# Forgetting attention: both heads of a pair through a query block together, scores as K=64 products in two row groups

## What is computed

```
logits = einsum('bhqd,bhkd->bhqk', qi, k) * scale + Fi[..., :, None] - F[..., None, :]
logits = where(kpos[None, :] <= qpos[:, None], logits, -inf)
p = softmax(logits, axis=-1)
out = einsum('bhqk,bhkd->bhqd', p, v)          # per head, swept over query blocks
y_f = out.reshape(B, S, F_W) * silu(f_z)
```

## Time and profile before

| | |
|---|---|
| median of 3 runs | 1825.53 us (1823.52 to 1827.44) |
| profiled execution | 1827.74 us, span 1826.1 us, mean granted clock 0.964 |
| TensorE busy | 1700.4 us (93%) |
| TensorE weight loads | 1301.9 us (71%) |
| VectorE busy | 826.4 us (45%) |
| ScalarE busy | 490.5 us (27%) |
| attention stage | first score at 1033.65 us, last output store issued at 1539.26 us |

### The profile page before, as it was taken

The page is one execution under the profiler, slowest core; times in us unless marked ns, Lnnn a source line. Parts: engine busy times, 40 slices in busy tenths (PEclk is TensorE's granted clock), DMA queues, the critical chain, the costliest instruction groups (busy, mean ns, idle before and its releaser), DMA issues. The chain is left out here.

```text
span 1826.1 us, 24542 instructions
## 1 busy us (share of the span) xinstructions
PE 1700.4 (93%) x8650; PEld 1301.9 (71%) x8650; DVE 826.4 (45%) x1819; ACT 490.5 (27%) x738; POOL 126.2 (7%) x122
## 2 busy tenths in 40 slices
PE   7689999999999999999998399999899996799998
PEld 6558888877777778888886266566565663688887
DVE  1942234221111134453111376566575664677774
ACT  1611011100010012221000255455454553322221
POOL 1610000000000000000000000000000000122221
PEclk9779999999999999999999699999999998799999
DMA  9520231321111111122111844506208101677762
GB/s 338 162 82 26 101 115 57 115 92 69 69 69 69 57 69 69 70 75 74 70 53 61 200 143 105 138 12 159 89 6 201 47 13 29 180 185 187 191 177 84
DMA packets 142094, 187.54 MB, mean 103 GB/s; under 512 B 9113, under 2 KB 116349, under 8 KB 135933
## 3 DMA queue, kind: packets, MB, share of 16 engines
q1 hardware_dynamic: 135252, 139.98, 27.8%
q0 software_dynamic: 6784, 46.89, 6.6%
HBM read 126.77 MB, written 60.06 MB: 102 GB/s over the span
## 5 line engine op out<-in xcount | busy, mean ns | idle before, releaser
L559 PE MATMUL a_ps_u<-a_h_hi,a_w_hi 128*128 128x512 f32 x1152 | 469.3, 407 | 0.0
L559 PE MATMUL a_ps_u<-a_h_lo,a_w_hi 128*128 128x512 f32 x1152 | 465.1, 404 | 0.0
L559 PE MATMUL a_ps_u<-a_h_hi,a_w_lo 128*128 128x512 f32 x1152 | 336.3, 406 | 0.0
L559 PEld LDWEIGHTS a_ps_u<-a_h_hi,a_w_hi 128*128 128x128 f32 x1152 | 216.6, 188 | 52.9 <-issue 1.9
L559 PEld LDWEIGHTS a_ps_u<-a_h_lo,a_w_hi 128*128 128x128 f32 x1152 | 216.7, 188 | 48.8
L559 PEld LDWEIGHTS a_ps_u<-a_h_hi,a_w_lo 128*128 128x128 f32 x1152 | 210.2, 188 | 51.2
L1213 DVE CUSTOM_DVE_ANT_0 f_probs<-f_ps_s,f_neg_f 128x512 f32<-128x512 f32 (+2 forms) x320 | 186.8, 608 | 130.3 <-PE f_ps_s L1101 80.4
L634 ACT ACTIVATE a_u_copy<-a_ps_u 128x2048 f32<-128x2048 f32 x28 | 52.8, 1886 | 462.9 <-PE a_ps_u L559 462.9
L1135 PE MATMUL f_ps_o<-f_probs_t,v_tok 128*64 128x512 f32 (+3 forms) x640 | 158.4, 559 | 13.4 <-ACT f_probs_t L1304 8.6
L1295 ACT ACTIVATE f_probs<-f_probs,f_neg_max 128x128 f32<-128x128 f32 (+15 forms) x128 | 153.5, 1199 | 54.5 <-DVE f_neg_max L1221 54.4
L1100 PE MATMUL f_ps_s<-k_hi,q_pack 128*128 128x512 f32 (+2 forms) x320 | 136.9, 428 | 19.3 <-DMA f_neg_f<-scratch_f_negF 13.4
(11 more groups left out here) (196 smaller groups left out, 1867.9 us busy)
## 6 DMA issues: line engine op xcount, KB each, us to landing
scratch_arrays<-a_stage POOLq DMA_DIRECT2D x27, 1024.0 KB, 4.2
a_w_land<-in_w_in SPq DMA_DIRECT2D x36, 512.0 KB, 3.8
scratch_qkT<-a_stage POOLq DMA_DIRECT2D x8, 2048.0 KB, 7.6
a_w_ring<-in_w_ada SPq DMA_DIRECT2D x12, 1024.0 KB, 9.0
a_x_ring<-in_x SPq DMA_DIRECT2D x16, 512.0 KB, 3.4
q_pack<-scratch_qkT SPq DMA_DIRECT2D x32, 256.0 KB, 7.5
k_hi<-scratch_qkT SPq DMA_DIRECT2D x32, 256.0 KB, 8.1
k_lo<-scratch_qkT SPq DMA_DIRECT2D x32, 256.0 KB, 8.6
```

The lines of the kernel that those rows point to most:

```text
L559: ins = pe.matmul(ps_u[:, par, b, :], w[:, k, :], h[:, k, cols], start=(k == 0 and i < 2 * len(blocks) and h is h_hi), stop=(k == KT - 1 a ...
```

## The change

Both heads of a pair now go through query group J together. Queries and keys lie as `q_hi`, `q_lo`, `k_hi`, `k_lo` with head 0 in partitions 0 to 63 and head 1 in 64 to 127. A chunk is scored for both heads by three products (high by high, low by high, high by low; the fourth term, low by low, is left out) of 64 rows each, one per head, in the two row groups and into two PSUM banks. A step is one key tile: both heads' blocks are turned, and both heads' products go to their own halves of the output bank, so nothing is folded. The inverse sums are spread over the 64 columns, turned once per group at step 2, multiplied by the gate, and applied to the output bank by one multiply. `ps_t` has three single banks, `ps_s` two slots of two; who copies a block is set by `taken_on_vector`. `plan` and `exp_plan` spread scores and exponentials of the next group over the steps. `probs` of even groups lie partly in the buffer of the output weights, whose load moves to the last group of the last pair. The core of the diff:

```
+def load_fox_qk(sp, scratch, fox, row, half):
     cols = slice(half * SEQ // 2, (half + 1) * SEQ // 2)
-    for part in range(2):
-        rows = slice(part * F_DH, (part + 1) * F_DH)
-        for name, source, first in (("q_pack", part, row), ("k_hi2", 0, row + F_W), ("k_lo2", 1, row + F_W)):
-            sp.dma_start(fox[name][rows, h, cols].bitcast(F32), scratch["qkT"][source, bass.ds(first, F_DH), cols]
-                         ).then_inc(fox["head_landed"][h][half], 16)
+    for name, source, first in (("q_hi", 0, 0), ("k_hi", 0, F_W), ("q_lo", 1, 0), ("k_lo", 1, F_W)):
+        sp.dma_start(fox[name][:, cols].bitcast(F32),
+                     scratch["qkT"][source, bass.ds(row + first, P), cols]).then_inc(fox["qk_landed"][half], 16)
+FOX_QK_LOADS = 4
...
+        SLOTS = 2
+        T_BANKS = 3
...
+        def probs(J, h, r, cols):
...
+            if J % 2:
+                return probs_long[:, h, r, cols]
+            i = h * QT + r
+            if i < IN_W:
+                return w_flat[:, i * SHORT + cols.start:i * SHORT + cols.stop]
+            return probs_short[:, i - IN_W, cols]
...
+        probs_t = sb("probs_t", [P, 2, HP, NB])
+        inv_wide = sb("inv_wide", [P, QT, HP, F_DH])
+        inv_z = sb("inv_z", [P, NB])
...
+        STEPS = [(J, kt) for J in range(GROUPS) for kt in range(key_tiles(J))]
...
+        USES = [use for J, kt in STEPS for use in
+                [("probs", J, kt, 0), ("probs", J, kt, 1)] + ([("inverse", J, None, None)] if kt == INV_AT else [])]
...
+        def taken_on_vector(use):
+            kind, J, kt, h = use
+            return kind == "inverse" or (h == 1 and (J == GROUPS - 1 or (J and kt % 2 == 1)))
...
+        def taken(eng, n, u):
+            if taken_on_vector(USES[u]):
+                eng.wait_ge(taken_by_dve, n * BY_DVE + FIRST_DVE + by_dve(u + 1))
+            else:
+                eng.wait_ge(copied_by_act, n * BY_ACT + FIRST_ACT + by_act(u + 1))
...
+        def plan(J, last_pair):
+            n = key_tiles(J)
+            following = [] if J + 1 == GROUPS and last_pair else chunks((J + 1) % GROUPS)
+            begin, end = (n // 3, n - 3) if J + 1 == GROUPS else (0, n - 1 if J == 0 else n - 2.5)
+            cuts = [min(len(following), max(0, math.ceil(len(following) * (p - begin) / (end - begin)))) for p in range(n)]
+            cuts.append(len(following))
+            cuts[0] = 0
             return [list(enumerate(following))[cuts[p]:cuts[p + 1]] for p in range(n)]
-        def columns_of(J, kt):
-            return max(0, kt - QT * J) * P
+        def exp_plan(J, last_pair):
+            shares, waiting, out = plan(J, last_pair), [], []
+            for p, share in enumerate(shares):
+                left = len(shares) - 1 - p
+                count = len(waiting) if left == 0 else max(1, -(-len(waiting) // left))
+                out.append(waiting[:count])
+                waiting = waiting[count:]
+                rows = [(r, h, c * NB + width) for m, (r, c, width, last) in share if last for h in range(HP)]
+                waiting += rows
+            out[-1] += waiting
+            return out
...
-                sp.wait_ge(s_used, n * ALL_CHUNKS + S_BANKS + chunks_before(LAST - 1))
-                load_head(0, n + 1)
+                sp.wait_ge(s_used, HP * (n * N_CHUNKS + SLOTS + N_CHUNKS))
+                for half in range(2):
+                    load_fox_qk(sp, scratch, fox, n * P + P, half)
+                    load_neg_f(n + 1, half)
                 store_y(n, GROUPS - 2)
-                sp.wait_ge(s_used, n * ALL_CHUNKS + S_BANKS + chunks_before(LAST))
-                load_head(1, n + 1)
+                taken(sp, n, inverse_at(GROUPS - 1))
+                load_fox_z(sp, scratch, fox, n + 1)
                 for half in range(2):
-                    sp.wait_ge(pv_done, n * ALL_PAIRS + 2 + pairs_before(LAST - 1, (half + 1) * TT // 4))
+                    sp.wait_ge(pv_done, n * N_STEPS + 2 + first_step(GROUPS - 1) + (half + 1) * TT // 2)
                     load_fox_v(sp, scratch, fox, half, n + 1)
                 store_y(n, GROUPS - 1)
-                load_fox_z(sp, scratch, fox, n + 1)
-            for J in range(GROUPS):
-                store_y(PAIRS - 1, J)
+            n = PAIRS - 1
+            for J in range(GROUPS - 1):
+                store_y(n, J)
+            sp.wait_ge(t_psum, n * len(USES) + use_at(GROUPS - 1, 0, 0))
+            sp.dma_start(w_land[:, :, :], a["w_out"][0].rearrange("(k p) n -> p k n", p=P)).then_inc(w_landed, 16)
...
-                def scores(g, m, r, c, width, last):
-                    h, J = ORDER[g % LAST]
+                def scores(n, J, m, r, c, width, last):
+                    at = chunks_before(J) + m
                     if m == 0 and J * NB % (SEQ // 2) == 0:
...
-                    pe.wait_ge(s_used, n * ALL_CHUNKS + S_BANKS + last_of_bank(g, m) + 1)
-                    q = q_pack[:, h, (J * QT + r) * P:(J * QT + r + 1) * P]
+                        pe.wait_ge(qk_landed[J * NB // (SEQ // 2)], (n + 1) * FOX_QK_LOADS * 16)
+                    pe.wait_ge(s_used, HP * (n * N_CHUNKS + at + 1))
+                    rows = slice((J * QT + r) * P, (J * QT + r + 1) * P)
                     keys = slice(c * NB, c * NB + width)
-                    bank = ps_s[:, bank_of(g, m), :]
-                    pe.matmul(bank[:, 0:width], q, k_hi2[:, h, keys], start=True, stop=False)
-                    ins = pe.matmul(bank[:, 0:width], q, k_lo2[:, h, keys], start=False, stop=not last)
+                    banks = [ps_s[:, at % SLOTS, h, :] for h in range(HP)]
+                    for q, k in ((q_hi, k_hi), (q_lo, k_hi), (q_hi, k_lo)):
+                        for h in range(HP):
+                            own = slice(h * F_DH, (h + 1) * F_DH)
+                            ins = pe.matmul(banks[h][:, 0:width], q[own, rows], k[own, keys],
+                                            start=(q is q_hi and k is k_hi), stop=(k is k_lo and not last))
+                            if k is k_lo and not last:
+                                ins.then_inc(s_psum, 1)
                     if last:
-                        ins = pe.matmul(bank[:, width - P:width], ident_r[:, :], mask_r[:, :], start=False, stop=True)
-                    ins.then_inc(s_psum, 1)
...
+                        for h in range(HP):
+                            pe.matmul(banks[h][:, width - P:width], ident_r[:, :], mask_r[:, :], start=False, stop=True
+                                      ).then_inc(s_psum, 1)
...
+                def turn(n, J, kt):
+                    for h in range(HP):
+                        u = use_at(J, kt, h)
+                        if kt == 0 and h == 0:
+                            pe.wait_ge(exp_ready, n * N_ROWS + (J + 1) * QT * HP)
+                        taken(pe, n, u - T_BANKS)
+                        for r in range(columns_of(J, kt) // P, QT):
+                            ins = pe.transpose(ps_t[:, u % T_BANKS, r * P:(r + 1) * P],
+                                               probs(J, h, r, slice(kt * P, (kt + 1) * P)), ident[:, :])
+                        ins.then_inc(t_psum, 1)
+                    if kt == INV_AT:
+                        u = inverse_at(J)
+                        pe.wait_ge(wide_ready, n * GROUPS + J + 1)
+                        taken(pe, n, u - T_BANKS)
+                        for r in range(QT):
+                            ins = pe.transpose(ps_t[:, u % T_BANKS, r * P:(r + 1) * P],
+                                               inv_wide[:, r].rearrange("p h d -> p (h d)"), ident[:, :])
+                        ins.then_inc(t_psum, 1)
...
+                def product(n, J, kt):
+                    at = first_step(J) + kt
+                    for h in range(HP):
+                        taken(pe, n, use_at(J, kt, h))
                     for half in range(2):
-                        if h == 0 and 2 * p == half * TT // 2 and J == half * TT // 2 // QT:
+                        if kt == half * TT // 2 and J == kt // QT:
                             pe.wait_ge(v_landed[half], (n + 1) * 16)
-                    if p == 0:
-                        pe.wait_ge(ot_ready, n * LAST + g + 1)
-                        pe.wait_ge(x_used, n * X_READS + x_reads_before(g) + 1)
-                    for e in range(2):
-                        kt = 2 * p + e
-                        first = columns_of(J, kt)
-                        ins = pe.matmul(ps_o[e * F_DH:(e + 1) * F_DH, first:], v_tok[:, kt, h, :],
-                                        probs_t[:, at % 2, e, first:], start=(p == 0), stop=(p == pairs(J) - 1))
+                    if kt == 0:
+                        pe.wait_ge(y_ready, n * GROUPS + J + 1)
+                    first = columns_of(J, kt)
+                    for h in range(HP):
+                        ins = pe.matmul(ps_o[h * F_DH:(h + 1) * F_DH, first:], v_tok[:, kt, h, :],
```

(71 more changed lines are left out.)

332 lines of the change are left out of this document (103 added, 229 removed).

## The result

The kernel after took 1852.95 us (median of 4 runs, 1851.12 to 1856.77) against 1824.93 of the kernel before (4 runs, 1823.52 to 1827.44): ratio 1.0155 [1.0135, 1.0175]. The forecast was 1850, in a range of 1797 to 1890. The profiled execution after spans 1849.5 us against 1826.1.

A forecast was written before the change was run, and what follows sets the result against it. TensorE was taken to bound the attention stage. Per pair, work saves 6.6 us but waits and clock rise from 10.6 to 25.3: +32 for four pairs, loads -4, end -3, so +25, 1850 us, range 1797 to 1890.

The forecast's parts named there:

- The mechanism: Block starts in attention: transposes wait for all eight exponentials, 6.3, 5.6 and 3.4 us, together 15.3 per pair.
- Work after: TensorE's scores, masks, transposes, products and shape changes in the changed attention stage: 108.3 us per pair of heads.
- rival B: Score products: row groups don't overlap, 4 x 23.3 = 93 us on the forecast, 1943 us; chance 0.08.
- Work before: TensorE's attention work in the old kernel: 114.9 us per pair of 125.5 observed, 10.6 being waits and lost clock.
- Clock: Behind the three longer idles per pair TensorE gets the lower clock: 2 us lost each, 6 per pair, bounds 0 and 10.
- The pair's edge: Between pairs of heads: TensorE's idle behind VectorE stays 2.5 us; VectorE's changed operations add nothing.
- Start: First pair's loads: 1 MB less ahead of the last small store, stage begins earlier, minus 4 us (bounds 0 and 8).
- End: Stage end: copy, fold, multiply and turning back before the last output multiply go, minus 3 us.
- Rival A: Block ends: TensorE's waits are half the forecast's and the clock holds, 29 us faster, 1797 us; chance 0.26.
- C: Whole stage: gain of 6.6 and shorter ends met by 7 to 9 us more waits per pair, about 1826; chance 0.06.
- D: Score products: the skill's row-tiling loss (3.07 times, not 4) adds 24 us, 1874; chance 0.60 together with the forecast.

The follow-up runs named there:

- e4: Kernel after with two full-array (K=128) score products in place of three in row groups, results differ: 1853.93 us.
- e7: Kernel after with each query and key load cut into two halves of 64 partitions, same bytes: 1854.49 us.
- e3: Kernel after with exponentials of 128 columns instead of up to 2048, without scale and maximum: 1790.08 us.
- e2: Kernel after with a new block's transposes waiting row by row and head by head for their own exponential, not all eight: 1831.31 us.
- e1: Kernel after with the plan running every ready exponential at once instead of spreading them over the steps left: 1840.7 us.
- e10: Kernel after with both heads' score products reading head 0's rows, so both use one row group: 2017.11 us.

## Why the prediction was right, and where not

- **The mechanism held.** Twelve waits of a new block's transposes for the exponentials, three a pair: forecast 6.3, 5.6 and 3.4 us, measured 5.68, 5.03 and 2.31. (By its own durations the forecast's second and third end at 8.3 and 7.2 us and not 8.0 and 7.0, 2 us in four pairs.) Taking the exponentials' length away took 63 us away with it.
- **Work after: 108.3 a pair forecast, 108.7 measured** (434.6 / 4). The sum is confirmed, not each of its terms. Two products at once, nearly free: shown by the records and by the single row group, whose added work was 87 us for 93 forecast in rival B. B's 1943 missed the clock, so it would have been 2017.
- **Work before was sized too low.** I counted 114.9 a pair and called the other 10.6 waits and lost clock. These are 7.7, (22.8 + 8.0) / 4, and the work is 118.5. So the work saved is 9.9 a pair and not 6.6: 13 us better than forecast in all. The miss is not in the row groups: with their masks and changes of shape the forecast had them save 0.6 a pair (6.9 less, 1.3 and 5.0 more), and e4 shows 0.25. It is in the rest, 6.0 forecast and 9.6 measured.
- **Clock: right at the block waits, left out elsewhere.** Forecast 6 a pair, measured 9.7. The twelve block waits cost 6.7 a pair, 2.2 each for 2 forecast: the lower level lasts 6.8 or 10.2 us at the long ones and 3.4 at those of 2.31. The other 3.0 are the edges (6.7 in all) and the stage's start (5.3). The forecast had seen the clock at the edge, some 3 us of work, and did not carry it into its sum for the kernel after. With the idle time of 17.2 a pair (19.3 forecast: 15.3 + 2.5 + 1.5) it makes 26.9 for 25.3.
- **The pair's edge: "nothing" was wrong.** I left 2.5 us as it was. It became 4.86 and 4.16 at the first two edges (the third, where the loop has ended, has none), and with its clock is worth 13 us. Of VectorE I had priced the operations and not the time between the loop's end and its first instruction.
- **Start: -4 forecast.** The first score came 11.4 us earlier. The first logits, at 1027.02 for 1034.74, came only 7.7 earlier: VectorE waits there for f_neg_f, 4.8 us. The bytes ahead on the queue were counted about right (e7: 6 us for 5); their number, 2.4 us, was not counted.
- **End: -3 forecast**, is not separated from the work by any run.
- **Rival A (1797).** Its waits did not halve, but it is where the change goes without them: 1790 in e3. **C (1826)** needed half the added waits; e2, with 49.7 left of the 76.8 us of added idle time and clock, is at 1831 and near it. **D (1874)** did not show. The Trainium skill's measured speedup of 3.07 for four row groups ("TensorE: Matmul & The Clock Gate", Part 3) gave an estimate of 6 us a pair; here a pair in the middle of a chunk takes 0.23, as one product over the full array does, and the loss sits in the changes of shape.

The total came out 3 us from the median because the misses cancel. Between the two traces the change is 23.4 us for 25 forecast: the work, with the end, is 10 us better than forecast, the start 7, the stage behind 2, and idle time and clock are 18 worse (76.8 added, 59 forecast: 4 times 14.7). Part of this is no luck. The stage before was measured as a whole, so the work that I left out of it (3.6 a pair, 14 in all) went into its waits, and the two errors had to meet. That the clock which the forecast left out and the earlier start, which it had too small, about balance is luck.

What stays open: why VectorE's edge is 4.83 us after and 2.66 before for the same loop form. That writing it out removes it is shown; that VectorE waits there for its instructions is only supported by the traces, as above, and why their load starts later in the kernel after is not known. Nor did any run take the clock's fall alone away, so that its price rests on the split above, and on e1, whose runs lie 11 us apart with the granted clock (0.954 at 1830, 0.946 to 0.949 at 1840).

## What to carry to other kernels

When a change makes one engine wait for a group of results, list what the other engine still has to do at that moment and put the clock behind it on the bill: here 46 us more of idle time came with 31 more of lost clock. Wait for the row that the next instruction needs, and let the planner finish the rows that somebody waits for first. When work saved is off by a remainder, size the remainder from the trace (idle, low clock) before calling what is left waits.

## What the runs showed that I had not expected

- Two row groups each ran their own products whatever the order in the code: three of head 0 and then three of head 1 still start in pairs, 10 ns apart.
- With one row group in use for the scores, the lower clock held for 20.5 us at waits of about 5 us and for 47.8 at the edges, with TensorE busy for 88% of it or more (18.13 of 20.50 in one); with two in use, 3.4 to 10.2. At waits of 2.3 us it was 3.4 us in the kernel after as well as in e10.
- From a chunk's first mask to its second it took 0.164 us behind row-group products and 0.060 behind full-array ones; the first pair behind another shape took 0.33 instead of 0.23.
- VectorE's return to the head of a long loop left it without work for 2.7 to 4.8 us, and TensorE behind it: 10 us in the kernel before and 13 in the kernel after, gone when the loop was written out. In every trace with the loop VectorE went on 2.1 to 2.3 us after a load of instructions had started.
